# adaLN weight tiles in a two-layer fp32 encoder kernel: from one tile per transfer to two tiles per transfer

## The reference, cut to what matters

```
cond = silu(c)                                              # 1024 values
mod = (cond @ ada_w[layer] + ada_b[layer]).reshape(9, 1024) # ada_w[layer]: 1024 x 9216
h = modulate(rmsnorm(x), shift, scale)
x = x + 0.5 * gate * swiglu(h, w13, w2)                     # w13: 1024 x 5632, w2: 2816 x 1024
```

## Time and profile before

| | |
|---|---|
| median of the runs shown | 977.48 us |
| the profiled execution itself | 978.21 us |
| its span, first to last instruction | 976.2 us |
| PE busy | 932.6 us (96%) |
| DVE busy | 704.0 us (72%) |
| POOL busy | 107.7 us (11%) |
| data moved | 239 MB, 245 GB/s on average |

### The profile page before, as it was taken

The page is one execution under the profiler, slowest core; times in us unless marked ns, Lnnn a source line. Parts: engine busy times, 40 slices in busy tenths (PEclk is TensorE's granted clock), DMA queues, the critical chain, the costliest instruction groups (busy, mean ns, idle before and its releaser), DMA issues.

```text
span 976.2 us, 11122 instructions
## 1 busy us (share of the span) xinstructions
PE 932.6 (96%) x4302; PEld 752.0 (77%) x4302; DVE 704.0 (72%) x693; ACT 447.3 (46%) x617; POOL 107.7 (11%) x177
## 2 busy tenths in 40 slices
PE   3799999999998899999999999999999899999998
PEld 1478788887776777887888878878878778888886
DVE  4786978976887758786888677868765878554534
ACT  2364434344646747534424365344453474342421
POOL 1001211100341110011111000111110000000000
PEclk9899999999998999999999999999999999999999
DMA  9999999686753249899999458986784398556221
GB/s 311 368 318 381 379 338 315 227 269 172 267 166 102 91 157 291 306 333 341 317 332 336 158 180 295 335 272 228 261 277 170 125 340 289 167 173 200 87 86 44
DMA packets 149141, 239.26 MB, mean 245 GB/s; under 512 B 16225, under 2 KB 108129, under 8 KB 148961
## 3 DMA queue, kind: packets, MB, share of 16 engines
q1 hardware_dynamic: 129360, 169.11, 51.9%
q0 software_dynamic: 18864, 69.21, 19.9%
q10 hardware_dynamic: 864, 0.23, 0.1%
HBM read 237.48 MB, written 1.05 MB: 244 GB/s over the span
## 4 chain that ended last, share of the span: by engine, by line
PE 79%; DVE 9%; issue 3%; ACT 2%; DMA 2%; POOL 2%; SPq 2%; DVEq 0%; ACTq 0%
PE ps L1597 48%; PE ps L1656 8%; PE ps L1657 8%; PE ps L1660 8%; DMA raw<-in_ff_w 2%; PE ps L1632 2%; DVE lo L1048 1%; DVE xn L1177 1%; POOL rstd L594 1%; PE ps L1690 1%; DVE x L1181 1%; PE ps L1670 1%; DVE acc L1108 1%; SPq L475 1%; PE ps L1589 1%
## 5 line engine op out<-in xcount | busy, mean ns | idle before, releaser
L1597 PE MATMUL ps<-hi,hT_hi 128*128 128x512 f32 (+1 forms) x848 | 339.3, 400 | 8.2 <-DVE hT_lo L1219 5.2
L1597 PE MATMUL ps<-hi,hT_lo 128*128 128x512 f32 (+1 forms) x848 | 330.6, 390 | 0.0
L1597 PE MATMUL ps<-lo,hT_hi 128*128 128x512 f32 (+1 forms) x848 | 330.4, 390 | 0.0
L1597 PEld LDWEIGHTS ps<-hi,hT_hi 128*128 128x128 f32 x848 | 160.4, 189 | 47.6 <-issue 15.5
L1048 DVE TENSOR_TENSOR lo<-raw,hi 128x2048 fp32r<-128x2048 f32 (+1 forms) x75 | 167.0, 2230 | 30.0 <-ACT hi L685 29.9
L1597 PEld LDWEIGHTS ps<-hi,hT_lo 128*128 128x128 f32 x848 | 160.4, 189 | 33.9
L1597 PEld LDWEIGHTS ps<-lo,hT_hi 128*128 128x128 f32 x848 | 160.6, 189 | 32.0 <-issue 1.4
L685 ACT ACTIVATE hi<-raw 128x2048 fp32r<-128x2048 f32 (+1 forms) x74 | 139.9, 1891 | 16.4 <-DMA raw<-in_w_in 8.4
L578 POOL DMA_DIRECT2D ada<-in_ada_w x128 | 68.9, 539 | 503.1 <-DVE acc L1108 199.6
L1108 DVE SCALAR_TENSOR_TENSOR acc<-ada,cond,acc 128x1024 f32<-128x1024 f32 x70 | 89.7, 1281 | 4.1 <-DMA ada<-in_ada_w 0.8
L1048 DVE TENSOR_TENSOR lo<-arena,hi 128x2048 fp32r<-128x2048 f32 x32 | 73.2, 2288 | 16.9 <-ACT hi L685 16.9
(11 more groups left out here) (190 smaller groups left out, 1007.9 us busy)
## 6 DMA issues: line engine op xcount, KB each, us to landing
raw<-in_ff_w SPq DMA_DIRECT2D x200, 512.0 KB, 5.7
ada<-in_ada_w POOLq DMA_DIRECT2D x128, 512.0 KB, 6.4
arena<-in_ff_w SPq DMA_DIRECT2D x64, 512.0 KB, 5.9
raw<-in_w_in SPq DMA_DIRECT2D x24, 512.0 KB, 4.9
arena<-in_ada_w SPq DMA_DIRECT2D x4, 1024.0 KB, 12.0
raw<-in_w_out SPq DMA_DIRECT2D x8, 512.0 KB, 4.1
ada<-in_ada_w SPq DMA_DIRECT2D x2, 1024.0 KB, 8.7
raw<-in_ada_w SPq DMA_DIRECT2D x2, 1024.0 KB, 14.7
```

The costliest lines, as they stand in the source:

```text
L1597: ins = mm(out, a, b, start=first and m == 0, stop=last and m == len(pairs) - 1, skip_group_check=shared)
```

## The change

POOL issues two neighbouring tiles as one transfer of 1 MB. The four places become two places of two tiles: j steps by two, the transfer writes `slot` and `slot + 1`, and there are two `ada_in` semaphores in place of four. Before it issues tiles n and n + 1, POOL now waits until tile n - 3 has been used, since both places must be free. DVE waits for the semaphore of the two-tile place at the first as at the second tile. What DVE computes and its order are unchanged.

```diff
@@ -374,7 +374,7 @@
-        ada_in = [sem(f"ada_in{i}") for i in range(ADA_RING)]
+        ada_in = [sem(f"ada_in{i}") for i in range(ADA_RING // 2)]
@@ -435,7 +435,7 @@
-            engine.wait_ge(ada_in[j % ADA_RING], 16 * ((KT * g + j) // ADA_RING - 3))
+            engine.wait_ge(ada_in[j // 2 % (ADA_RING // 2)], 16 * ((KT * g + j) // ADA_RING - 3))
@@ -568,15 +568,15 @@
-                for j in range(first, last):
-                    n = KT * g + j
+                for j in range(first, last, 2):
+                    n, slot = KT * g + j, j % ADA_RING
                     if n >= 2 * KT + ADA_RING:
-                        pool.wait_ge(ada_used, ada_count(*divmod(n - ADA_RING, KT)))
+                        pool.wait_ge(ada_used, ada_count(*divmod(n + 1 - ADA_RING, KT)))
...
-                    pool.dma_start(ada[:, j % ADA_RING, :], ada_v[layer][:, j, v * D:(v + 1) * D]
-                                   ).then_inc(ada_in[j % ADA_RING], 16)
+                    pool.dma_start(ada[:, slot:slot + 2, :], ada_v[layer][:, j:j + 2, v * D:(v + 1) * D]
+                                   ).then_inc(ada_in[slot // 2], 16)
```

## The result

The changed kernel takes 981.35 us (median of 20 runs, 977.96 to 988.48), the kernel before 977.16 us (20 runs, 975.14 to 981.13). The ratio is 1.0046 (95% interval 1.003 to 1.0062): some 4.5 us more, 0.46% (4.2 us between the medians). The loss is clear of noise; it lies just inside 0.5%, and its interval reaches past that. 981.0 was forecast.

The account below looks back on a forecast made before the run. PE, busy 932.6 us, was taken to set the time. Fewer issues gave 0, the stall at tile 24 +3.3 us, elsewhere nothing: 981.5 against the profiled execution, 980.8 on the median, stated as 981.0; range 977.5 to 990.

Parts of the forecast that it names:

- Half as many issues, 0: On POOL, 128 ada issues of 0.54 us become 64; POOL's time is off the path, so this gives 0.
- The landing of 1 MB: A two-tile transfer lands 1.7 us after one tile would: 8.8 us when issued at 91.55, 9.6 at 103.27.
- Tile 24 is 3.3 us late: In ffn(0), tile 24's pair lands at 100.4 where DVE started the tile at 97.10: 3.3 us late.
- PE's wait there goes from 1.18 to 4.5 us: Before the second matrix near 98 us, PE waits for u_low behind tile 24, moving by the full 3.3 us.
- rival (D): Later, fewer issues let SP's second-matrix load through before tile 24: at most -1.2 us; chance 0.10 shared with two other rivals.
- a second matrix that lands at another time than 86 us: Sign that the forecast is wrong at tile 24, since all there hangs on DVE's being late for this load.
- Elsewhere it is covered: Beyond tile 24 other tiles come 0.3 to 3.9 us late, but DVE's spare time prevents a second PE stall.
- the walk: DVE's queue stepped through from tile 24 with late landings, moving PE when u_mul, u_low or a finished vector comes late.
- Rival (B): Ring starves DVE; PE waits for u_low repeatedly in ffn(0) and ffn(1) from 9.3 us landings; 986 to 996 us, chance 0.37.

## Why the prediction was right, and where it was not

**Half as many issues, 0.** Right. An issue now takes 0.72 us on POOL in place of 0.54 (46.2 us for 64 in place of 68.9 for 128), and POOL still waits 498.5 us.

**The landing of 1 MB.** Forecast 8.8 and 9.6 us for the pairs of tiles 24 and 28. Measured for these two, issued at 88.5 and 103.3:

```profile
DMA to landing us min/median/max: 8.6/8.6/8.6
...
DMA to landing us min/median/max: 9.4/9.4/9.4
```

The rule "as one tile lands there, and 1.7 us for the second" held to 0.2 us, though both pairs were issued some 3 us earlier than forecast (91.55 and 106.6). The Trainium skill, "DMA: Bandwidth & Descriptors", section on the anatomy of one DMA, gives 2.0 us plus bytes over 436 GB/s, which makes an estimate of 4.4 us for 1 MB. The trace does not agree: the shortest landing of a pair here was 5.3 us, the median 7.7, beside SP's loads, and the trace decides.

**Tile 24 is 3.3 us late.** 2.99, 2.78 and 2.70 in three profiles. Right.

**PE's wait there goes from 1.18 to 4.5 us.** This term was too large: 2.48 and 2.58 in the two profiles of the changed kernel, 3.55 only where pair 24 is alone. What failed is that DVE's being late ahead of tile 24 was carried over unchanged; its easing stood only as rival (D), with 1.2 us as the most. With 1.18 us of waiting before and a tile 2.99 us late, 4.2 us were due; 2.48 were seen, so 1.7 us came back. Net, the stall adds 1.3 to 1.4 us of idle time in these profiles. Where pair 24 alone was changed and DVE's wait stayed at 6.82 us, the tile was 2.70 us late and PE's wait grew by 2.4: there the forecast's step holds. The prediction named the sign, a second matrix that lands at another time than 86 us, and it showed. ACT's start on that load, before and after:

```profile
85.95 1.06 ACT L768 ACTIVATE hi<-raw 128x1024 fp32r<-128x1024 f32 x1 [8.48 <-DMA raw<-in_ff_w]
```
```profile
82.91 1.06 ACT L768 ACTIVATE hi<-raw 128x1024 fp32r<-128x1024 f32 x1 [6.69 <-DMA raw<-in_ff_w]
```

Of these 3.0 us, 1.25 are a general shift (PE was ready for its second matrix at 96.06 in place of 97.31) and 1.8 are DVE's shorter wait. That the later issue of tiles 20 and 22 brought it is likely and not shown.

**The clock behind the wait.** The forecast lets a microsecond of PE's wait cost a microsecond; a term for the clock was missing. PE waited near 98 us for 1.18 us (before), 2.48 (after) and 2.56 (pairs to 55) with no stretch at 1.2 GHz behind it; for 2.58 with one of 3.4 us, and for 3.55 and 5.77 with one of 6.8 us. 2.56 and 2.58 us lie too close for the length of the wait alone to have decided. The forecast of 981.0 met the 981.35 although only 1.3 of the forecast 3.3 us of added idle time stand in the profiles; the rest of the measured loss goes, at least in part, with a lower clock that the forecast left out. The place, the cause and the sign are shown; the closeness of the number is luck.

**Elsewhere it is covered.** Right in the main: 3.24 us late at tile 28 (3.5 forecast), 0.8 us to spare (0.3), DVE waiting 34.1 us in all (30 to 40), no PE wait in ffn(1). The late tiles were six in ffn(0) and nine in ffn(1), where the walk had eight and ten. Pairs from 56 on at 0.9999 and pairs from 26 on at 1.0008 show it in time.

**Rival (B).** It stayed out, and when it was forced the walk gave twice what was measured. Its weight of 0.37 was too high. The walk takes one landing for all pairs, and they differ: the 14 pairs issued from 115 to 207 us landed in 5.4 to 8.5 us. In ffn(1) two pairs, issued at 468.8 and 472.0, took 10.2 us, more than the 9.3 from which the walk has PE stall again and again, and PE did not wait: single long landings were covered. Why the landings vary isn't shown.

**What stays open.** Ratios of 1.0029 for pair 24 alone, 1.0035 for the pairs of ffn(0) and 1.0045 for all agree within their intervals; whether pairs from 26 on add up to 2 us more isn't settled. That a longer wait brings the lower clock is shown by putting the wait in; how much of the loss is clock (about half, by the two groups of executions) rests on the sorting of executions, and executions with a low clock occur in kernels without the wait as well. Of the 2 us that stand with the clock high, the profiles show 1.3.

## What to carry to other kernels

A ring of n places refilled two at a time loses one place of lead for every even tile and lands it later; whether that costs is decided by what stands behind the late tile in the consumer's queue. Look for the one spot where the bound engine already waits a little for that queue: there each microsecond can count in full or more, elsewhere 30 us of waiting were free here. Where such a spot exists, moving the step that the bound engine needs ahead of the step that may be late is the cheaper cure: moving one call took the whole loss away here.

## What the runs showed of the hardware

I had not expected the clock. Waits of PE of 1.18, 2.48 and 2.56 us near 98 us left it at 2.4 GHz; with waits of 2.58, 3.55 and 5.77 us there went 3.4, 6.8 and 6.8 us at 1.2 GHz, and with the one of 3.61 us at 540 us 3.4 us. At 5.77 us that made 6.3 us (by the medians) out of 4.6 us of added wait. The length of a wait alone does not decide: near 271 us (a wait for `split_lo`) PE waits 1.95 to 2.27 us in ten of the 14 profiles, with 3.4 us at 1.2 GHz behind it in five of them and none in the other five (2.22 us with, 2.25 us without). Such stretches are there in kernels without any wait near 98 us too. Nor had I expected that DVE's wait for SP's load would be 5.45 us in place of 7.25 in the kernel in which POOL issues its tiles later; that one causes the other isn't shown.
